# Diagonal state space: its small matrices made early behind GpSimd's splits, saved in DRAM, and a deeper order of the steps

## What is computed

```
x[t] = a * x[t-1] + B u[t]
y[t] = real(C x[t]) + D * u[t]
out  = gelu(y)
```

## Time and profile before

| what | value |
|---|---|
| median of three executions | 2547.27 us (2543.61 to 2556.06) |
| the profiled execution, its own time | 2559.21 us |
| its span | 2557.5 us |
| busy, share of the span | PE 93%, PEld 71%, DVE 57%, ACT 28%, GpSimd (POOL) 57% |

### The profile page before, as it was taken

One profiled execution on the slowest core, in us unless ns is written; L12 is line 12 of the kernel. 1 busy time (PEld: TensorE's weight loads), 2 busy tenths in 40 slices (PEclk: granted clock), 3 DMA queues, 4 the chain that ended last, 5 costly groups with the idle time before them and its releaser, 6 DMA issues.

```text
span 2557.5 us, 33867 instructions
## 1 busy us (share of the span) xinstructions
PE 2377.8 (93%) x12614; PEld 1818.2 (71%) x12614; DVE 1459.5 (57%) x1960; ACT 703.7 (28%) x1170; POOL 1463.2 (57%) x1266
## 2 busy tenths in 40 slices
PE   5998989899999998887999999999988799999998
PEld 4865755467777776453786778888867688888887
DVE  6888822167787856454455376661349726666223
ACT  2032112234444412222214222220146403222101
POOL 4820355455454562454562376667789467666774
PEclk9988799999999998998999999999999999999999
DMA  7867689623333234996231133332421133333231
GB/s 293 284 187 242 254 321 367 211 78 111 108 90 107 90 140 171 384 377 238 79 99 33 36 97 98 98 95 90 124 70 34 50 83 99 98 96 93 95 103 66
DMA packets 297566, 370.23 MB, mean 145 GB/s; under 512 B 43792, under 2 KB 238416, under 8 KB 297200
## 3 DMA queue, kind: packets, MB, share of 16 engines
q1 hardware_dynamic: 243088, 309.20, 36.2%
q10 hardware_dynamic: 26576, 31.10, 3.7%
q0 software_dynamic: 27792, 28.40, 3.3%
HBM read 406.78 MB, written 36.25 MB: 173 GB/s over the span
## 4 chain that ended last, share of the span: by engine, by line
PE 27%; POOL 26%; issue 21%; DMA 14%; DVE 9%; ACT 1%; SPq 1%; POOLq 0%; ACTq 0%; DVEq 0%
POOL WL L866 17%; POOL WH L862 6%; PE PAIR L527 5%; PE PAIR L528 5%; PE PAIR L529 5%; DMA XG<-htok_scratch,GATHER_I 4%; DMA RAW<-in_ffn_w_up 3%; PE BANK L1837 3%; DMA y_scratch<-OG,SCATTER_I 2%; PE BANK L2278 1%; DMA ADA_A<-in_ada_w 1%; PE PAIR L1861 1%; DMA ADA_B<-in_ada_w 1%; POOL EXTRA_W L2027 1%; PE PAIR L1823 1%
## 5 line engine op out<-in xcount | busy, mean ns | idle before, releaser
L866 POOL TENSOR_TENSOR WL<-RAW,WH 128x512 fp32r<-128x512 f32 x576 | 797.5, 1415 | 12.0
L527 PE MATMUL PAIR<-HH,WH 128*128 128x512 f32 x1792 | 707.6, 395 | 12.3 <-issue 3.7
L529 PE MATMUL PAIR<-HH,WL 128*128 128x512 f32 x1792 | 699.4, 390 | 0.0
L528 PE MATMUL PAIR<-HL,WH 128*128 128x512 f32 x1792 | 699.4, 390 | 0.0
L861 POOL TENSOR_TENSOR TURN<-ONES 128x1 f32<-128x1 f32 x144 | 35.0, 243 | 749.3 <-PE PAIR L529 708.3
L527 PEld LDWEIGHTS PAIR<-HH,WH 128*128 128x128 f32 x1792 | 337.4, 188 | 93.6 <-issue 16.3
L529 PEld LDWEIGHTS PAIR<-HH,WL 128*128 128x128 f32 x1792 | 337.5, 188 | 71.0
L528 PEld LDWEIGHTS PAIR<-HL,WH 128*128 128x128 f32 x1792 | 337.5, 188 | 70.5 <-issue 2.2
L862 POOL TENSOR_SCALAR WH<-RAW 128x2048 fp32r<-128x2048 f32 x144 | 282.7, 1963 | 0.0
L527 PE MATMUL PAIR<-FHH,WH 128*128 128x512 f32 x352 | 138.7, 394 | 0.0
L529 PE MATMUL PAIR<-FHH,WL 128*128 128x512 f32 x352 | 138.0, 392 | 0.0
(11 more groups left out here) (544 smaller groups left out, 4031.6 us busy)
## 6 DMA issues: line engine op xcount, KB each, us to landing
PAIR_W<-in_moe_w SPq DMA_DIRECT2D x96, 1024.0 KB, 11.1
RAW<-in_ffn_w_up SPq DMA_DIRECT2D x88, 512.0 KB, 5.0
ADA_B<-in_ada_w SPq DMA_DIRECT2D x30, 1024.0 KB, 5.4
RAW<-in_ssm_w_in SPq DMA_DIRECT2D x48, 512.0 KB, 4.9
ADA_A<-in_ada_w SPq DMA_DIRECT2D x18, 1024.0 KB, 9.0
RAW<-in_ffn_w_down SPq DMA_DIRECT2D x32, 512.0 KB, 4.3
RAW<-in_ev_w_in SPq DMA_DIRECT2D x20, 512.0 KB, 4.8
RAW<-in_mix_in_units SPq DMA_DIRECT2D x16, 512.0 KB, 7.5
```

The costliest lines, as they stand in the source:

```text
L527: nc.tensor.matmul(o, wh, xh, start=start, stop=False)
L528: nc.tensor.matmul(o, wh, xl, start=False, stop=False)
L529: return nc.tensor.matmul(o, wl, xh, start=False, stop=stop)
L866: ins = pool.tensor_tensor(WL[:, s, c], RAW[:, s, c], WH[:, s, c].bitcast(F32), ALU.subtract)
```

## The change

GpSimd makes W1 for all eight steps during the way in: behind each split of its units 2 to 9 stands one `pool_s5_inputs`, and its result is saved to `w1_dram` by a DMA from GpSimd's queue. Its last of four parts is now a copy, since the power 0 is one, so products and sums have 192 elements. BB is loaded again ahead of that by GpSimd's queue. C is laid out by the host and loaded straight into CK by GpSimd's queue, which waits for it; behind each split of the first 16 units of feed forward 0 stands one half (real or imaginary) of `pool_s5_outputs`, and every second time a save to `ca_dram`. PE's turning of C and ACT's copies go. DVE waits for the saves before attention 1 (whose buffers hold the W1 work) and before unit 15 of feed forward 0 (whose tiles lie over the CA work); for that the loop of `dve_ffn` is cut in two, in both layers. In the state space stage SP loads W1_AT and CA_AT of each step. The rows U4 of all eight steps have a place of their own. PE gathers and turns step k+2 ahead of the y products of step k, and ACT's order follows. DVE's loop over the steps is written out. The diff leaves out the tiles' places, the removed functions for C, the numbers of the banks and the host's layout of C.

```diff
+    W1_NEW = S1[:, 1, 0:1024].rearrange("p (a i t j c) -> p a i t j c", a=2, i=2, t=4, j=S5_L)
+    W1_TMP = [a.rearrange("p (t j c) -> p t j c", t=4, j=S5_L) for a in (S1[:, 1, 1024:TRI], PT1[:, 1, 1024:TRI])]
+    BB = PT1[:, 1, 0:1024].rearrange("p (i t c) -> p i t c", i=2, t=S5_TILES)
...
-        with dve.loop(FB // 2 - 1, {w["conv_in"]: 4, w["gate"]: 2, w["hidden"]: 2, w["hidden_hi"]: 2, dve.chain: 2}) as i:
-            for u in (1, 2):
-                scale(i, u)
-                low(i, u - 1)
-                convolve(i, u)
+        for first, last in ((1, CA_TILE - 1), (CA_TILE - 1, FB - 1)):
+            if layer == 0 and first > 1:
+                for par in range(2):
+                    dve.e.wait_ge(matrix_saved[par], 16 * KD)
+            with dve.loop((last - first) // 2, {w["conv_in"]: 4, w["gate"]: 2, w["hidden"]: 2, w["hidden_hi"]: 2, dve.chain: 2}) as i:
+                for u in (first, first + 1):
+                    scale(i, u)
+                    low(i, u - 1)
+                    convolve(i, u)
...
+        def matrices(k):
+
+            par = k % 2
+            if k >= 2:
+                sp.wait_ge(w["w1x"], k - 1)
+                sp.wait_ge(w["ca"], k - 1)
+            sp.dma_start(W1_AT[:, par].rearrange("p i t j c -> p (i t j c)"), w1_dram[k]).then_inc(matrix_landed[par], 16)
+            sp.dma_start(CA_AT[:, par].rearrange("p i t j c -> p (i t j c)"), ca_dram[k]).then_inc(matrix_landed[par], 16)
+
         if first == 0:
-            engine.wait(w["spilled"], 16)
             for par in range(2):
                 engine.wait(turn_saved[par], 8 * KD)
-            sp.dma_start(BB[:].rearrange("p a t c -> p (a t c)"), bb_dram).then_inc(w["reloaded"], 16)
+                engine.wait(matrix_saved[par], 16 * KD)
+            matrices(0)
+            matrices(1)
+        else:
+            matrices(first)
         for k in range(first, last):
             par = k % 2
+            if first and k + 1 < KD:
+                matrices(k + 1)
             if k >= 2:
                 sp.wait_ge(w["state"], k - 1)
             sp.dma_start(TURNING[:, par].rearrange("p a t n -> p (a t n)"), turn_dram[k]).then_inc(turn_landed[par], 16)
...
+    def pool_s5_load_b(pool):
+
+        pool.wait(s5_sems["spilled"], 16)
+        pool.e.dma_start(BB.rearrange("p i t c -> p (i t c)"), bb_dram).then_inc(s5_sems["reloaded"], 16)
+
     def pool_s5_inputs(pool, k):
         w, par, tiles = s5_sems, k % 2, slice(4 * k, 4 * k + 4)
-        shape = lambda a: bcast(a, 2, S5_L)
+        if k == 0:
+            pool.wait(w["reloaded"], 16)
+        if k >= 2:
+
+            pool.e.wait_ge(matrix_saved[par], 16 * (k // 2))
+        last = S5_L - 1
+        shape = lambda a: bcast(a, 2, last)
         br, bi = (shape(BB[:, i, tiles, :]) for i in range(2))
-        ar, ai = (bcast(A_REV[:, i, :, tiles].rearrange("p j t -> p t j"), 3, S5_C) for i in range(2))
-        if k >= 2:
-
-            pool.e.wait_ge(w["w1x"], k - 1)
-        q = [W1_PR[:, par, i] for i in range(4)]
-        for i, (a, b) in enumerate(((br, ar), (bi, ai), (br, ai), (bi, ar))):
-            ins = pool.e.tensor_tensor(q[i], a, b, ALU.mult)
+        ar, ai = (bcast(A_REV[:, i, 0:last, tiles].rearrange("p j t -> p t j"), 3, S5_C) for i in range(2))
+        real, imag = (W1_NEW[:, par, i, :, 0:last, :] for i in range(2))
+        one, two = (a[:, :, 0:last, :] for a in W1_TMP)
+        for o, a, b in ((real, br, ar), (one, bi, ai), (imag, br, ai), (two, bi, ar)):
+            ins = pool.e.tensor_tensor(o, a, b, ALU.mult)
         pool.link(ins)
-        pool.e.tensor_tensor(q[0], q[0], q[1], ALU.subtract)
-        pool.e.tensor_tensor(q[2], q[2], q[3], ALU.add).then_inc(w["w1_sums"], 1)
+        pool.e.tensor_tensor(real, real, one, ALU.subtract)
+        pool.e.tensor_copy(W1_NEW[:, par, :, :, last, :], BB[:, :, tiles, :])
+        pool.e.tensor_tensor(imag, imag, two, ALU.add).then_inc(w["w1_sums"], 1)
         pool.wait(w["w1_sums"])
-
-    def pool_s5_outputs(pool, k):
+        pool.e.dma_start(w1_dram[k], W1_NEW[:, par].rearrange("p i t j c -> p (i t j c)")).then_inc(matrix_saved[par], 16)
+
+    def pool_s5_load_c(pool):
+
+        pool.e.dma_start(CK[:], t["od_c_rows"].rearrange("p (a t c) -> p a t c", a=2, c=S5_C)).then_inc(s5_sems["landed"], 16)
+        pool.wait(s5_sems["landed"], 16)
+
+    def pool_s5_outputs(pool, k, part):
         w, par, tiles = s5_sems, k % 2, slice(4 * k, 4 * k + 4)
         cr, ci = (bcast(CK[:, i, tiles, :], 2, S5_L + 1) for i in range(2))
         ar, ai, an = (bcast(a[:, :, tiles].rearrange("p j t -> p t j"), 3, S5_C) for a in (A_POW[:, 0], A_POW[:, 1], A_NEG))
-        if k >= 2:
-
-            pool.e.wait_ge(w["ca"], k - 1)
-        q = [PRP[:, par, i] for i in range(4)]
-        for i, (a, b) in enumerate(((cr, ar), (ci, ai), (cr, an), (ci, ar))):
-            ins = pool.e.tensor_tensor(q[i], a, b, ALU.mult)
-        pool.link(ins)
-        pool.e.tensor_tensor(q[0], q[0], q[1], ALU.subtract)
-        pool.e.tensor_tensor(q[2], q[2], q[3], ALU.subtract).then_inc(w["ca_sums"], 1)
+        if k >= 2 and part == 0:
+
+            pool.e.wait_ge(matrix_saved[par], 8 * KD + 16 * (k // 2))
+        new, tmp = CA_NEW[:, par, part], CA_TMP[:, part]
+        pool.e.tensor_tensor(new, cr, (ar, an)[part], ALU.mult)
+        pool.link(pool.e.tensor_tensor(tmp, ci, (ai, ar)[part], ALU.mult))
+        pool.e.tensor_tensor(new, new, tmp, ALU.subtract).then_inc(w["ca_sums"], 1)
         pool.wait(w["ca_sums"])
+        if part:
+            pool.e.dma_start(ca_dram[k], CA_NEW[:, par].rearrange("p i t j c -> p (i t j c)")).then_inc(matrix_saved[par], 16)
+
+    def pool_s5_matrices(pool):
+
+        pool_s5_load_b(pool)
+        for k in range(KD):
+            split_unit(pool.e, plan.u["evin"] + 2 + k)
+            pool_s5_inputs(pool, k)
+        split_units(pool.e, plan.u["evout"], plan.u["ffn0"])
+        pool_s5_load_c(pool)
+        for u in range(CA_TILE):
...
-    def pe_s5_prepare(pe, k):
+    def pe_s5_inputs(pe, k):
 
         w, par = s5_sems, k % 2
-        if k == 0:
-            pe_s5_turned(pe, 0)
-        if k == 0:
-            pe.wait(h_ready)
-        if k == 1:
-            b = factor_bank(PLAIN)
-            pe.e.wait_ge(bank_free[b % 4], b // 4 + 1)
-        pe_s5_u_rows(pe, k)
-        if k:
-            pe_s5_turned(pe, k)
         pair = take_pair(pe, plan.p["s5"] + k)
...
+    def pe_s5_kernel(pe, k):
+
+        w, par = s5_sems, k % 2
         pe.wait(w["ca"])
...
     def pe_s5(pe):
-        pe_s5_prepare(pe, 0)
+        pe_s5_turned(pe, 0)
+        pe.wait(h_ready)
+        pe_s5_u_rows(pe, 0)
+        pe_s5_inputs(pe, 0)
+        pe_s5_kernel(pe, 0)
+        b = factor_bank(PLAIN)
+        pe.e.wait_ge(bank_free[b % 4], b // 4 + 1)
+        pe_s5_u_rows(pe, 1)
+        pe_s5_turned(pe, 1)
         for k in range(KD):
-            if k < KD - 1:
-                pe_s5_prepare(pe, k + 1)
+            if k + 1 < KD:
+                pe_s5_inputs(pe, k + 1)
+                pe_s5_kernel(pe, k + 1)
+            if k + 2 < KD:
+                pe_s5_u_rows(pe, k + 2)
+                pe_s5_turned(pe, k + 2)
             pe_s5_output(pe, None, k)
...
     def act_s5_u_rows(act, k):
-        par, b = k % 2, s5_a(k, "u")
-        if k >= 2:
-
-            act.e.wait_ge(bank_ready, s5_y(k - 2) + 1)
-        act.e.activation(U4[:, par].rearrange("p t n -> p (t n)"), full_bank(act, b)[:], ACT.Copy).then_inc(bank_free[b % 4], 1)
+        b = s5_a(k, "u")
+        act.e.activation(U4[:, k].rearrange("p t n -> p (t n)"), full_bank(act, b)[:], ACT.Copy).then_inc(bank_free[b % 4], 1)
...
     def act_s5_w1_blocks(act, k):
         w, par = s5_sems, k % 2
-        act.wait(w["w1_sums"])
+        if k == 0:
+            act.e.wait_ge(w["w1_sums"], KD + 1)
+        act.wait(matrix_landed[par], 32)
         if k >= 2:
 
             act.e.wait_ge(bank_ready, s5_a(k - 2, "kernel") + 1)
...
     def act_s5_decay(act, k):
@@ -3448,12 +3484,17 @@
         if k >= 2:
 
             act.e.wait_ge(w["state"], k - 1)
+        for i in range(4):
+            ins = act.e.activation(S5_DECAY[:, par, i, :], FIRST[:], ACT.Identity, scale=S5K[:, MAG4, 4 * k + i:4 * k + i + 1])
+        ins.then_inc(w["decays"], 1)
+
+    def act_s5_skip(act, k):
+        w, par = s5_sems, k % 2
+        if k >= 2:
+
             act.e.wait_ge(bank_ready, s5_a(k - 2, "kernel") + 1)
         act.e.activation(SKIP[:, par], IDENT[:], ACT.Identity, scale=COLS[:, col_at["od_d"] + k:col_at["od_d"] + k + 1])\
             .then_inc(w["skip"], 1)
-        for i in range(4):
-            ins = act.e.activation(S5_DECAY[:, par, i, :], FIRST[:], ACT.Identity, scale=S5K[:, MAG4, 4 * k + i:4 * k + i + 1])
-        ins.then_inc(w["decays"], 1)
...
     def act_s5(act):
         w = s5_sems
         act_s5_w1_blocks(act, 0)
         act_s5_turned(act, 0)
         act.wait(w["consts"])
         act_s5_ca_blocks(act, 0)
+        act_s5_skip(act, 0)
```

(41 more changed lines are left out.)

84 lines of the change are left out of this document (31 added, 53 removed).

## The result

The changed kernel takes 2554.61 us (median of 20 runs, 2548.81 to 2562.91), the kernel before in the same series 2550.35 us (20 runs, 2542.10 to 2556.06): ratio 1.0023, 95% interval 1.0014 to 1.0032, so 3.6 to 8.2 us slower (the two medians are 4.3 us apart). Forecast were 3 us fewer. The difference is within the 0.5% called no change, but it has the other sign, and the interval leaves zero out. A second series gave 1.0026 (1.0010 to 1.0041).

The account below looks back on a forecast made before the run. In the state space stage DVE, slowed beside GpSimd, was to give way to a PE-ACT ring of 14.4 us a step. Terms -8 + 4 + 1 = -3 us gave 2544 us; own range 2537 to 2552, wide range 2528 to 2556.

Parts of the forecast that it names:

- -8 + 4 + 1: Forecast changes in us: state space stage -8, way in +4, start of feed forward 0 +1; sum -3.
- the wide range: Whole kernel: 2528 to 2556 us, the forecast's own range plus most of the first rival and the third.
- the third rival: State space stage keeps its time, as landed loads or ACT are late; insertions cost 5; 2552 us, chance 0.10.
- The ring of 14.4 us: State space step: inputs and kernel 4.07, semaphores 0.4, ACT 8.1, output turn 1.84; y(7) 9 us earlier.
- 1 us for the whole stage: State space stage: 1 us taken back for y products at half clock after waits, making 9 us earlier -8.
- The deeper order: State space stage: PE does u and turned of step k+2 before y(k), ACT's order follows; within the -8 us.
- If ACT did not hold Y, the gain is 15: State space stage, bound of the -8 us: the ring is then PE's 13.2 us, the gain 15.
- The way in, +4: Way in: insertions of 4.4 us on GpSimd make PE wait for splits of units 8 and 9; bounds 0 and 16.
- Feed forward 0, +1: Start of feed forward 0: GpSimd's wait for C delays its first split, some DVE contention; +1 us, bounds 0 and 6.
- The DVE chain of this norm gets some contention: Start of feed forward 0: GpSimd slows DVE's norm chain somewhat; no size of its own, inside the +1 us.
- The slower rival: GpSimd's splits become the bound in the way in and first 16 feed forward units: +17, 2564 us, chance 0.08.
- rule of a full block: Feed forward units: exclusive lock blocks the loser a whole instruction; insertion 4.3 us, 16 end 12 us late; not adopted.

Follow-up runs that it names:

- moving the call: Against the changed kernel, ACT copies Y ahead of the W1 matrices of three steps on; alone 2540.44 us, ratio 0.9972 to the kernel before.

## Why the prediction was wrong

The sum was -8 + 4 + 1. By the means of all profiles that share the code it is **-2.3 + 4.7 + 4.4 = +6.8 us**; the attention, 88.7 us before, is at 86 to 87 in most profiles of changed kernels and at 88.7 in three, which takes up to 2.4 us off. Measured are 3.6 to 8.2. The time lies in the wide range, near its upper end, and outside the forecast's own (2537 to 2552); that it lies in the wide one says nothing for the mechanism, since the forecast was for a faster kernel and this one is slower. The nearest case was the third rival (the stage keeps its time, the insertions cost 5: 2552 us), which had 0.10, with insertions that cost 9.

- **The ring of 14.4 us, the step that failed.** Its mechanism held: ACT works 8.1 us from the start of the kernel's copy to the end of Y's (1960.49 to 1968.63; forecast 8.1), PE waits for Y 1.9 to 2.5 us in each of the first five steps ("about 2" was forecast), VectorE's operations with two SBUF inputs are back at 0.69, and its wait for HH, 37.7 us in 7, shows that it is no bound. Two terms were off. The output turn was taken at 1.84 us, the piece of it ahead of the rows of u; up to the inputs, which now follow it, it is 2.4 (1968.77 to 1971.14): 14.85 us a step. Only three of the five steps counted have that length, the first takes 16.13 us and the fifth, with no W1 copy left, 13.16, so together the five are 73.8 us where 72.3 were forecast. The greater miss is the clock: I took 1 us for the whole stage, where a low stretch costs up to 1.6 us, and the profiles have two to four of them, 5.5 us on average. 8 less 1.5 and 4.5 is 2, and the mean of the profiles is 2.3.
- **The deeper order was credited without a comparison.** The old order without GpSimd was never worked out. It runs at 14.42 us, so the new one at 14.4 would have had nothing to give but its start. The prediction's own rows said so: 13.1 us and a wait of 1.3 for W_T are 14.4, the pace of the kernel before wherever VectorE keeps up. The wait of 11.7 us for W_T was no gain by itself, as Y then held PE for longer.
- **Bounds.** "If ACT did not hold Y, the gain is 15": moving the call gave 16.4, 15.4, 16.4 and 15.9.
- **The way in, +4: 4.7 measured**, an insertion 4.4 us as forecast. The wait was placed wrongly: not units 8 and 9 waiting for WL by 4 us (0.9 us), but VectorE's gating products, slowed by the later split.
- **Feed forward 0, +1: 3.8 to 5.8 measured.** The wait for C was right (0.60 + 4.44 us; 5 for the landing and 0.79 for the issue were forecast; the 3.2 us given beside them is too short for this load) and makes unit 0 1.3 us late. "The DVE chain of this norm gets some contention" is the other failed step: it was named, had to share 1 us with the wait for C, and by subtraction cost 2.5 and more, the low clock behind its wait included; no run separates the two. Behind unit 4 nothing more is lost, as forecast, though GpSimd waits for PE only once there (1.2 us).
- **The slower rival** priced an insertion in the way in at 6.9 us and GpSimd's splits as the bound. That isn't what happened: PE waits for WL 0.9 us in the way in and 0.5 in the feed forward units. The kernel is slower by VectorE's chains and by the clock. Of the Trainium skill's rule of a full block (SBUF — State Buffer, "Who interferes with whom"), the feed forward units show nothing late; where a chain of VectorE is tight, the rows of 1.78 and 2.40 us are nearer to the rule than the 1.0 that I carried over from the stage.

## What to carry to other kernels

A wait that a reordering removes is worth what the next releaser in the ring allows: write the engine's new order down, call by call, and put the copy that another engine waits for ahead of work that is needed three steps later. Work moved into GpSimd's pauses was free only where VectorE had no tight chain with two SBUF inputs at that moment; look at what VectorE does there, not at how long GpSimd waits. Before a new order of steps is priced, price the old order under the same conditions. And compare stages between the same two marks: here two whole profiles differed by 10 us in the wrong direction, from parts that nobody had changed.
